# Head norms of keys and of the last query tile through sums by token, the other sums between the pieces of the next tile

## The reference

```python
k = rmsnorm(kv[..., :hkv].reshape(B, T, N_KV_HEADS, HEAD_DIM), k_norm)
...
q = rmsnorm(x, P['b_norm'][j]) @ P['w_q'][j] + P['b_q'][j]
q = rmsnorm(q.reshape(B, T, N_HEADS, HEAD_DIM), P['q_norm'][j])
...
scores = einsum(q, k) * HEAD_DIM ** -0.5 + bias ; softmax with a sink ; times v
```

## Time and profile before

| | us |
|---|---|
| three runs | 2592.06, 2589.78, 2589.05 (median 2589.78) |
| the profiled execution, its own time | 2591.95 |
| its span | 2589.9 |
| TensorE (matmul) busy | 2479.5 |
| VectorE busy | 1303.8 |
| ScalarE busy | 783.2 |
| GpSimd busy | 243.6 |
| mean granted TensorE clock | 0.982 of full speed |

### The profile page before, as it was taken

One profiled execution on the slowest core, in us unless ns is written; L12 is line 12 of the kernel. 1 busy time (PEld: TensorE's weight loads), 2 busy tenths in 40 slices (PEclk: granted clock), 3 DMA queues, 4 the chain that ended last, 5 costly groups with the idle time before them and its releaser, 6 DMA issues.

```text
span 2589.9 us, 39596 instructions
## 1 busy us (share of the span) xinstructions
PE 2479.5 (96%) x15088; PEld 2409.6 (93%) x15088; DVE 1303.8 (50%) x2064; ACT 783.2 (30%) x1259; POOL 243.6 (9%) x352
## 2 busy tenths in 40 slices
PE   5899889999999999999999889999999999999998
PEld 4899889999999999999988855999999999999998
DVE  7566664553453344345467676355425534533542
ACT  4454443220231221112334467233112212311111
POOL 2011322000000000000311044210000000000000
PEclk7999989999999999999999988999999999999999
DMA  3111011111111111111151310111111111111112
GB/s 112 41 41 39 26 42 41 49 35 48 48 44 37 54 44 36 53 40 41 49 83 39 95 54 2 33 50 40 39 51 49 34 47 48 42 39 52 45 37 85
DMA packets 222510, 121.92 MB, mean 47 GB/s; under 512 B 24541, under 2 KB 220061, under 8 KB 222332
## 3 DMA queue, kind: packets, MB, share of 16 engines
q1 hardware_dynamic: 220180, 117.18, 15.6%
q10 hardware_dynamic: 2196, 3.74, 1.2%
q0 software_dynamic: 64, 0.05, 0.0%
HBM read 112.30 MB, written 10.55 MB: 47 GB/s over the span
## 4 chain that ended last, share of the span: by engine, by line
PE 86%; DVE 6%; issue 3%; ACT 2%; DMA 2%; POOL 1%; SPq 0%; ACTq 0%; DVEq 0%; POOLq 0%
PE ps L708 27%; PE ps L710 27%; PE ps L709 27%; PE ps L998 1%; DMA raw<-in_w_q 1%; PE ps L1050 1%; PE ps L895 1%; DVE wlo L1521 0%; PE ps L743 0%; DVE y L1549 0%; DVE y L1689 0%; DVE y L1687 0%; DVE t L1973 0%; DVE y L1953 0%; DVE pb L1953 0%
## 5 line engine op out<-in xcount | busy, mean ns | idle before, releaser
L708 PE MATMUL ps<-sa,whi 128*128 128x384 f32 (+1 forms) x1836 | 605.0, 330 | 33.1 <-issue 18.0
L710 PE MATMUL ps<-sa,wlo 128*128 128x384 f32 (+1 forms) x1836 | 602.9, 328 | 0.0
L709 PE MATMUL ps<-sa,whi 128*128 128x384 f32 (+1 forms) x1836 | 602.5, 328 | 0.0
L708 PE MATMUL ps<-sb,whi 128*128 128x384 f32 (+1 forms) x1800 | 592.0, 329 | 5.7 <-DVE sb L2027 3.8
L710 PE MATMUL ps<-sb,wlo 128*128 128x384 f32 (+1 forms) x1800 | 587.9, 327 | 0.0
L709 PE MATMUL ps<-sb,whi 128*128 128x384 f32 (+1 forms) x1800 | 587.4, 326 | 0.0
L1120 ACT ACTIVATE whi<-raw 128x1024 fp32r<-128x1024 f32 (+2 forms) x220 | 208.2, 946 | 881.4 <-PE ps L710 874.2
L708 PEld LDWEIGHTS ps<-sa,whi 128*128 128x128 f32 x1836 | 347.4, 189 | 37.1 <-issue 30.7
L708 PEld LDWEIGHTS ps<-sb,whi 128*128 128x128 f32 x1800 | 338.3, 188 | 10.8 <-issue 7.2
L709 PEld LDWEIGHTS ps<-sa,whi 128*128 128x128 f32 x1836 | 347.5, 189 | 0.5 <-issue 0.2
L710 PEld LDWEIGHTS ps<-sa,wlo 128*128 128x128 f32 x1836 | 347.6, 189 | 0.0
(11 more groups left out here) (316 smaller groups left out, 2389.6 us busy)
## 6 DMA issues: line engine op xcount, KB each, us to landing
raw<-in_f_w_up SPq DMA_DIRECT2D x96, 512.0 KB, 3.8
raw<-in_f_w_down SPq DMA_DIRECT2D x64, 384.0 KB, 3.5
raw<-in_a_w_in SPq DMA_DIRECT2D x16, 512.0 KB, 4.0
xrows<-in_x_prompt SPq DMA_DIRECT2D x8, 512.0 KB, 6.4
raw<-in_a_w_out SPq DMA_DIRECT2D x8, 512.0 KB, 4.2
raw<-in_w_q SPq DMA_DIRECT2D x16, 256.0 KB, 3.6
raw<-in_w_o SPq DMA_DIRECT2D x32, 128.0 KB, 2.9
strip<-strip_sb ACTq DMA_DIRECT2D x1, 3072.0 KB, 33.3
```

The costliest lines, as they stand in the source:

```text
L708: pe.matmul(out, whi[s][:, w], mhi[k][:, chunk(c)], start=(k == 0), stop=False)
L709: pe.matmul(out, whi[s][:, w], mlo[k][:, chunk(c)], start=False, stop=False)
L710: last = pe.matmul(out, wlo[s][:, w], mhi[k][:, chunk(c)], start=False, stop=(k == nk - 1))
```

## The change

1. Keys (tiles 0 and 1) and the last query tile (tile 9 in the numbering of the sums: two key tiles, then eight query tiles) get their sums by token: `token_stat` loads the squares of 128 tokens as weights and multiplies by two columns, nine times a tile, so that 18 numbers per partition hold all means (tokens on partitions). ScalarE takes their root (`token_root`) and VectorE their reciprocal (`token_inverse`) in one small instruction each. `spread` brings them back to channels on partitions: for each chunk six matmuls whose weights are one column repeated 64 times and whose moving side is the identity. VectorE multiplies straight from PSUM (`spread_norm`).
2. The spreads of the keys stand behind the first three pieces of the first query pair, two each, and VectorE's `spread_norm` of the keys behind the whole norm of x.
3. `place_free` says when a bank may be overwritten. The sums of the other query tiles stand between the pieces of a later tile (`q_stats`).
4. The state jobs stand behind pieces 1, 3, 4 and 5 of the values (before: 3, 4, 5 and the first query piece). State copies 4 and 5 move behind step 3 of the second chunk of `norm_hi`, 6 and 7 behind step 7.
5. Before the scores TensorE only does jobs 0 to 9 and two spreads. Jobs 10 and 11 and the third spread come behind `scores(0)`, jobs 12 and 13 behind `scores(1)`, with their copies on ScalarE and VectorE.

```diff
+            def token_stat(i):
+                pe.wait_ge(hsq, i + 1)
+                for b, t0 in enumerate(TOKENS):
+                    last = pe.matmul(head_sums(i)[:, 2 * b:2 * b + 2], squares_of(i)[:, t0:t0 + P], blockones[:, 0:P:HD],
+                                     start=True, stop=True)
+                last.then_inc(hmean, 1)
+
+            def place_free(i, c):
+                if (i, c) in ((0, 0), (0, 1)):
+                    pe.wait_ge(fst_cp, STATE0[1])
+                    return
+                j, d = (i, c - 2) if c == 2 else (i - 1, c + 1)
+                if j in BY_TOKEN:
+                    pe.wait_ge(hnorm, norms_at(j) + d + 1)
+                else:
+                    pe.wait_ge(hroot, means_at(j) + d + 1)
+
+            def spread(i, c):
+                pe.wait_ge(hinv, BY_TOKEN.index(i) + 1)
+                place_free(i, c)
+                for b in range(3 * c, 3 * c + 3):
+                    o = TOKENS[b] - CHUNKS[c][0]
+                    for e in range(2):
+                        last = pe.matmul(spread_out(i, c)[HD * e:HD * e + HD, o:o + P],
+                                         hst[:, i % 2, 2 * b + e:2 * b + e + 1].broadcast_to([P, HD]), ident[:, :],
+                                         start=True, stop=True)
+                last.then_inc(hspread, 1)
...
             first_pair(N_KV, split_b, None, 2, kv_slots, split_done(1, 2))
-            pe.wait_ge(stat_sqrt, 9)
-            head_stat(0, 0)
-            pe.wait_ge(strip_cp, 1)
-            head_stat(0, 1)
...
                     q = 2 * c + s
                     if q == 0:
-                        head_stat(0, 2)
-                        head_stat(1, 0)
+                        pe.wait_ge(stat_sqrt, 9)
+                        pe.wait_ge(strip_cp, 1)
+                        token_stat(0)
+                        token_stat(1)
                     elif q == 1:
-                        head_stat(1, 1)
...
+                        pe.wait_ge(hroot, 2)
+                        state_job(0, 0)
+                        state_job(0, 1)
+                    elif q >= 3:
+                        state_job(0, 2 * (q - 2))
+                        state_job(0, 2 * (q - 2) + 1)
 
             def q_slots(q):
-                if q == 0:
-                    state_job(0, 6)
-                    state_job(0, 7)
+                if q < 3:
+                    for i, c in ((0, 2 * q), (0, 2 * q + 1)) if q == 0 else ((0, 2), (1, 0)) if q == 1 else ((1, 1), (1, 2)):
+                        spread(i, c)
+
+            def q_stats(t, c):
+                if t == 2:
+                    return ([(2, 0), (2, 1)], [(2, 2)], [(3, 0), (3, 1)])[c]
+                if t == 3:
+                    return ([(3, 2)], [(4, 0), (4, 1)], [(4, 2)])[c]
+                return ([(t + 1, 0), (t + 1, 1)], [(t + 1, 2)], [])[c]
 
             first_pair(N_Q, split_b, 1, None, q_slots)
-            pe.wait_ge(fst_cp, STATE0[1])
-            head_stats(2)
-            for t in range(2, KD - 1):
-                unit(N_Q + t // 2, t % 2, KD, split_b)
-                head_stats(2 + t - 1)
-            unit(N_O - 1, 1, KD, split_b)
+            for t in range(2, KD):
...
+                for c in range(3):
+                    piece(n, s, c, KD, split_b)
+                    for tile_, part in q_stats(t, c):
+                        head_stat(tile_, part)
...
-            head_stats(2 + KD - 1)
+            token_stat(2 + KD - 1)
 
             pe.wait_ge(ck_in, 16)
-            pe.wait_ge(hroot, 3 * (2 + KD))
-            for m in range(6, NPREP):
...
+            for m in range(6, NCK):
+                pe.wait_ge(prep_dve if m % 2 else prep_cp, (m - 6) // 2 + 1)
                 prep_job(m)
...
+            spread(2 + KD - 1, 0)
+            spread(2 + KD - 1, 1)
...
             scores(0)
+            prep_job(NCK)
+            prep_job(NCK + 1)
+            spread(2 + KD - 1, 2)
             scores(1)
+            for m in range(NCK + 2, NPREP):
...
+            def spread_norm(i, c):
+                dve.wait_ge(hspread, spreads_at(i) + c + 1)
+                root = spread_out(i, c)
...
+            for i in range(2):
+                token_inverse(i)
             dve.wait_ge(k_gap, 3)
 
-            dve.wait_ge(hmean, 3)
-            dve.wait_ge(hnorm, 2)
+            dve.wait_ge(hmean, 1)
             for c in range(3):
                 for s in range(2):
                     kv_out(1, s, c)
                 norm(1, C_BN, None, [c], split_b, lambda k: prep(N_Q, 0, KD * P) if (c, k) == (0, 6) else None)
                 if c == 0:
                     prep(N_Q, 1, KD * P)
+            for i in range(2):
+                for c in range(3):
+                    spread_norm(i, c)
```

More of the change, by code:

```diff
@@ L73 @@
 KB = WIN + 1
+TB = (T + P - 1) // P
+TOKENS = [min(P * b, T - P) for b in range(TB)]
+HCOL = 400
 KS = NB * KB
@@ L353, in norm_buffer, with squares_of, squares_free, means_at @@
             return convin[:, ds(8 + (i % 2) * 384, w)]
-        def root_buffer(i):
-            return rstd if i >= 3 and i % 2 == 1 else convin
+        def squares_of(i):
+            return ksq if i in (1, 2) or (i > 3 and i % 2 == 0) else y
+        def squares_free(i):
+            return {0: 0, 1: 0, 2: 2, 3: 1}[i] if i < 4 else means_at(i - 1)
+        BY_TOKEN = (0, 1, 2 + KD - 1)
+        def means_at(i):
+            return sum(1 if j in BY_TOKEN else 3 for j in range(i))
+        def norms_at(i):
+            return sum(3 if j in BY_TOKEN else 1 for j in range(i))
+        def spreads_at(i):
+            return 3 * BY_TOKEN.index(i)
+        def root_buffer(i):
+            return rstd if i % 2 else convin
+        N_HEADS = norms_at(2 + KD)
+        N_HEADS_A = norms_at(2 + KD // 2)
+        def head_sums(i):
+            return ps[:, 6 + i % 2, HCOL:HCOL + 2 * TB]
+        def spread_out(i, c):
+            return bank(6 + (3 * i + c) % 2, c)
         def job_out(job, bank_no):
@@ L887, in _ @@
             ffn(0, N_F0, split_b, sa, 0, 1)
+            def token_stat(i):
[23 more added lines that the diff above has]
+                last.then_inc(hspread, 1)
             def head_stat(i, c):
                 pe.wait_ge(hsq, i + 1)
-                if 3 * i + c >= 2:
-                    pe.wait_ge(hroot, 3 * i + c - 1)
-                src = ksq if i == 1 else y
-                pe.matmul(bank(6 + (3 * i + c) % 2, c), blockones[:, :], src[:, chunk(c)], start=True, stop=True)\
-                  .then_inc(hmean, 1)
-            def head_stats(i):
-                for c in range(3):
-                    head_stat(i, c)
+                place_free(i, c)
+                pe.matmul(spread_out(i, c), blockones[:, :], squares_of(i)[:, chunk(c)], start=True, stop=True)                  .then_inc(hmean, 1)
             def kv_slots(q):
@@ L1478, in _ @@
                     exps(n)
+                if n == 0:
+                    prep_out(range(NCK + 2, NPREP))
                 if n >= 2:
@@ L1914, in _, with prep_out @@
             dve.tensor_copy(sbias[:, :, 0:1], sinks_s[:, :].rearrange("p (g o) -> p g o", o=1)).then_inc(bias_sink, 1)
-            for m in range(1, len(jobs), 2):
+            def prep_out(m):
                 _, view, dst = jobs[m]
-                if m == 7:
-                    t = 2 + KD - 1
-                    for c in range(3):
-                        dve.wait_ge(hroot, 3 * t + c + 1)
-                        seq.mark(dve.reciprocal(root_buffer(t)[:, chunk(c)], root_buffer(t)[:, chunk(c)]))
                 dve.wait_ge(prep_tr, m + 1)
@@ L1925, in _ @@
                 dve.tensor_copy(dst, view).then_inc(prep_dve, 1)
+            for m in (1, 3, 5):
+                prep_out(m)
+            token_inverse(2 + KD - 1)
+            for m in (7, 9):
+                prep_out(m)
+            spread_norm(2 + KD - 1, 0)
+            spread_norm(2 + KD - 1, 1)
             def before_exp(i):
```

137 lines of the change are left out of this document (68 added, 69 removed).

## The result

The changed kernel is slower by 0.19%, a loss that the runs can tell from nothing, though it is smaller than the 0.2% that the prediction took as the least that can be told: 2595.6 us (median of 15 runs, 2591.67 to 2598.13) against 2589.89 (15 runs of the kernel before, 2587.57 to 2592.95); the ratio is 1.0019, 95% interval 1.0011 to 1.0027, and this interval does not reach 1. The profiled execution of the changed kernel took 2594.23, with a span of 2592.4 and a mean granted clock of 0.981.

What follows compares the result with a forecast made beforehand. TensorE, busy 2479.5 of 2589.9, was taken as the bound, through its work and idle stretches. 9.4 + 2.8 - 9.9 + 1.3 = +3.6 gave 2595.5 profiled, 2593.4 against the median; range 2587.0 to 2599.5.

Steps and rivals of the forecast that it cites:

- A: Values and first query pair, up to the start of query tile 2: loss 9.4, bounds 7.5 and 12.
- C: Last query piece to first scores: scores 13.4 behind that piece, gain 9.9, bounds 7.3 and 10.8.
- B: Query tiles 2 to 7: sums of seven tiles and not five stand there, loss 2.8, bounds 2 and 4.
- D: First steps of the softmax, with copies moved among the first exponentials and maxima: loss 1.3, bounds -1.5 and 4.
- the last piece of the values at 1356.6 ... so it costs nothing: Values: their last piece ends 0.6 before the transfer of 1357.20, so it costs nothing; beyond that, one for one.
- the release by that DMA: First query pair: whi (high weights) of slot 1 still released by its DMA near 1357, a sign of being right.
- The price of a record: Values: a token_stat record costs 0.12, between 0.06 and 0.19, so two token_stat of 36 records take 4.3.
- the one for copy 4: Ahead of state job 6: jobs 6 and 7 end at 1366.0; first two query pieces have some 2.1 of slack.
- the one for VectorE: First query pair: chunk 2's spread waits for spread_norm behind the whole norm of x; binding, third piece starts at 1379.8.
- 1 (half the clock): C and D at half the clock, if it is 0.5 when ck lands: +8.9 in all, 2598.7; chance 0.25.
- 2 (late values): Values: token_stat weight loads cost 0.19 a record, price +1.9, so +5.5, 2595.3; chance 0.10.
- 3 (an earlier DMA): First query pair: the transfer for slot 1's high weights lands before 1357.20; -4.1, 2585.7; chance 0.10.

Runs made afterwards that it cites:

- e1: Changed kernel with state copies 4 to 7 and state jobs 6 and 7 back in their order from before the change: 2597.99 us, ratio 1.0027.
- e3: Changed kernel with the edits of e1 and e2 both made (full name e3_both): 2587.06 us, ratio 0.9989.
- e8: Kernel of e3 with the four vp jobs and the last query tile's third spread put back ahead of the first scores: 2587.09 us, ratio 0.9987.
- e7: Kernel of e3 with 6.98 of whole-tile reciprocals put back on VectorE ahead of the last query tile's small reciprocal: 2587.38 us, ratio 0.9985.
- e9: Changed kernel with the sums of both key tiles done twice, 72 records and not 36: 2600.6 us, ratio 1.0042.
- e5_ck_first: Kernel of e3 with the DMA of ck issued ahead of the four of bias and not behind them: 2579.71 us, ratio 0.9965.
- e4: Changed kernel with the first key tile's sums ahead of the fourth values tile's first piece and not behind it: 2596.25 us, ratio 1.0019.
- e10: Kernel of e5_ck_first with two wide matmuls, read by nobody, where TensorE waits ahead of the fourth values tile: 2579.01 us, ratio 0.9958.
- e12: Kernel of e11_best with the wide matmuls of e10 and the two key tiles' sums apart, behind separate values pieces: 2580.08 us, ratio 0.9960.
- e11_best: Kernel of e5_ck_first with state copies 2 and 3 ahead of the high weights of slot 0 on ScalarE: 2581.95 us, ratio 0.9965.
- e2: Changed kernel with the six key spreads behind the third, fourth and fifth query pieces, not the first three: 2594.49 us, ratio 1.0015.

## Why the prediction was right, point by point

The forecast was no difference that can be told, 2593.4; 2595.6 lies in the range, and the ratio of 1.0019 is inside 0.2% by little. The 0.2% itself was too coarse: fifteen runs a side told a loss of 0.19%, to 0.08% either way. The path through the stage was as forecast. That the sum came out, +4.2 in the traces for +3.6, is in part luck: A and C were each 1.7 worse than said, B 0.9 and D 1.9 better. The terms, on the axis of before:

- *A, loss 9.4: measured 11.1* (67.83 and 78.92 from the last record ahead of the fourth values tile to query tile 2), inside its bounds. The mechanism held: copy 4 behind the norm's second chunk, the spread behind the norm. One step failed: "the last piece of the values at 1356.6 ... so it costs nothing". It ended at 1359.2, and the high weights of slot 1 started 2.05 later than in the kernel before, where their DMA had released them; the release by that DMA, which the text had named as a sign of being right, did not come. The price of a record was not the cause: 18 took 1.92, 0.107 each and not 0.12. The clock was: the two pieces took 1.5 more each, in a stretch for which the text had no half clock. That is 3.0 more, less 0.5 for the cheaper records, and the values are 2.5 late.
- Of the waits, the one for copy 4 was called hidden, with 2.1 of slack, and the one for VectorE binding. They are nearly a tie: TensorE waited 7.96 for copy 4, ran the first query piece at half the clock, and was left with 0.28 for the spread. e1 to e3 show what that is worth: neither edit gains, both together gain 8 to 9.
- *B, loss 2.8: measured 1.95*, a little under its bounds. The period became 13.67 and not 13.9 to 14. A unit without sums takes 12.07 (1458.35 to 1470.42 in the kernel before), so the sums of a tile cost 1.92 before, where 2.1 was assumed, and 1.65 now (from 82.01 and 83.96 between query tile 2 and the end of the last query piece). Seven at 1.65 less five at 1.92 is the 1.95.
- *C, gain 9.9: measured 8.2*, inside its bounds. `ck` landed 9.83 behind the last piece (9.0 assumed), and its transposes ran wholly at half the clock, 3.67 for 1.9; the spreads and the scores behind them had nearly the full clock again. e8 gives 4.3 of the gain to `vp`, e7 next to nothing to the reciprocals of the last tile; the part of the sums moved forward is what is left over, and not shown.
- *D, loss 1.3: measured a gain of 0.6* by the fourth scores (15.52 from the first to the fourth, 16.10 before). e8 shows why it is small either way.

11.1 + 1.95 - 8.2 - 0.6 = +4.2; 0.5 of that is the offset of the traces ahead of the stage, and another 1.2 was won back between the fourth scores and the projection of the outputs (whose first matmul the timelines have at 1615.63 and 1613.08), which leaves the 2.5 by which the spans differ. The median of the runs went up by 5.7; the profiled execution of the changed kernel is one of its shorter ones, that of the kernel before one of its longer ones.

Of the rivals, 1 (half the clock) came true in part. Its sign came in full, the clock was at 0.50 when `ck` landed, and so did the half clock in the first query piece, under cover as it said; but of its price of 5.3 in C and D only the 1.7 in C came, since the clock was back at 1.00 for the first scores and D gained. And the half clock also came in the values, where it had not been looked for. 2 (late values) had the right place and law, one for one as e9 shows, and the wrong cause. 3 (an earlier DMA) is out for the changed kernel: its values bind, not the transfer.

The rule of the Trainium skill on draining (TensorEngine Tiling (Array Packing), Key Properties) can be held against a row now. In e3_both two spreads stand between transposes and scores, 1.46 apart from their start to that of the next work (1487.50 to 1488.96) for 24 records; if the two changes of tile shape (into the spreads and out of them) drain TensorE, it is within that 1.46, and the prediction had taken 1.6 without it. No run here shows a price of the rule.

## What to carry to other kernels

Where two orders are changed ahead of the same stage, each may hide the wait of the other: undoing them one by one showed 2.8 lost (by the clock) and 0.3 won, undoing both 9.0. When a change leaves one DMA as the thing that is late next, look at once at what is issued ahead of it on its queue: here `ck` ahead of four bias transfers took the ratio from 0.9989 (e3_both) to 0.9965 (e5_ck_first), a kernel faster than both. It was not tried in the kernel before. Profile more than one execution before a difference of 1 to 3 is given a cause: the clock alone moved single places by as much. A matmul that moves two columns is cheap by itself, 0.107 at the full clock, but price what runs behind it at either clock.

## What was not expected of the hardware

- The granted clock fell to 0.50 not only after idle time but after busy TensorE with narrow work: behind 0.30 of idle time and 18 records that move two columns (e4), under or behind 36 such records with no idle time at all (e10; the changed kernel and every other one here with 36 in a row, the second piece 5.8 in each), and under 72 of them (e9). With the 36 in two parts, a piece of the values between them, it stayed at 1.00 (e12), and so it did with wide sums in the same place (kernel before). A piece costs 1.5 to 2.5 more each time. The Trainium skill (TensorE: Matmul & The Clock Gate, Part 1: The HAM clock gate) has activity lift the clock; these rows show that records of this kind, although the windows count TensorE busy for all of their time, do not hold it up.
- The same 16 transposes of `ck` behind the same wait of 1.6 ran at 1.00 in e5_ck_first and e10_wide_fill and at 0.50 in e11_best and e12_all. It is a difference of some 3 us in the first scores, and executions of e5_ck_first lie from 2578.15 to 2588.78. The same stands ahead of state job 4: behind one and the same wait of 2.51 its transposes took 1.08 in three kernels (changed, e3, e9) and 1.88 in seven (e1, e2, e4, e5, e7, e8, e10), and the values ended 1.3 later in these. What decides it was not found.
